# Expert layers: each result row goes straight to its token's place, and the finish reads plain blocks

## The reference, cut to what matters

```
g_val, g_idx = top_k(softmax(t @ w_group + b_group), 1)
e_val, e_idx = top_k(softmax(e_logits of that group), 2);  e_val /= sum(e_val)
weights, expert_id = g_val * e_val, g_idx * 4 + e_idx
hid = silu(t @ w_gate[e]) * (t @ w_up[e]) * combine[t, e]      # width 256
out = sum over the two experts of hid @ w_down[e]
h = layer_norm(alpha * h + out)
```

## Time and profile before

| | |
|---|---|
| median of the runs | 2432.27 us |
| the profiled execution, and its span | 2437.65 us, 2435.8 us |
| PE, DVE, ACT, POOL busy | 93%, 52%, 50%, 9% |
| software queue q0 | 17040 packets, 70.74 MB |
| hardware queue q1 | 50832 packets, 265.57 MB |
| first expert stage, steps | about 1632 to 1832 us |
| second expert stage, steps | about 2193 to 2402 us |

### The profile page before, as it was taken

One profiled execution on the slowest core, in us unless ns is written; L12 is line 12 of the kernel. 1 busy time (PEld: TensorE's weight loads), 2 busy tenths in 40 slices (PEclk: granted clock), 3 DMA queues, 4 the chain that ended last, 5 costly groups with the idle time before them and its releaser, 6 DMA issues.

```text
span 2435.8 us, 29892 instructions
## 1 busy us (share of the span) xinstructions
PE 2272.2 (93%) x11728; PEld 1089.1 (45%) x11728; DVE 1269.0 (52%) x2492; ACT 1224.4 (50%) x2127; POOL 223.7 (9%) x296
## 2 busy tenths in 40 slices
PE   7989999999999999999999999989996999989995
PEld 3333554444443444444444446544333444653333
DVE  5456855556445556776653684643115644653113
ACT  7543656666557566566665863531115664431113
POOL 0000000000000430000000000111221000111231
PEclk9999999999999999999999999989998999989998
DMA  5220011221222210222223231439974131427995
GB/s 194 86 98 9 1 69 70 104 104 72 90 107 79 97 69 36 88 103 104 82 77 131 74 103 54 192 119 384 406 300 156 74 139 39 161 103 310 415 420 234
DMA packets 68012, 338.22 MB, mean 139 GB/s; under 512 B 11702, under 2 KB 12012, under 8 KB 53516
## 3 DMA queue, kind: packets, MB, share of 16 engines
q1 hardware_dynamic: 50832, 265.57, 28.5%
q0 software_dynamic: 17040, 70.74, 7.7%
HBM read 366.62 MB, written 23.10 MB: 160 GB/s over the span
## 4 chain that ended last, share of the span: by engine, by line
PE 79%; DVE 10%; ACT 5%; DMA 3%; issue 3%; POOL 0%; SPq 0%; DVEq 0%; POOLq 0%; ACTq 0%
PE PB L383 11%; PE PB L388 11%; PE PB L389 11%; PE PB L3233 8%; PE PB L3259 4%; PE PB L1670 3%; PE PB L1666 3%; PE PB L1667 3%; PE PB L408 2%; PE PB L409 2%; PE PB L410 2%; PE PB L3185 1%; PE PB L419 1%; DVE WS L320 1%; ACT junk L261 1%
## 5 line engine op out<-in xcount | busy, mean ns | idle before, releaser
L388 PE MATMUL PB<-AS,WS 128*128 128x512 f16 x1416 | 537.0, 379 | 16.7 <-ACT AS L478 12.7
L389 PE MATMUL PB<-AS,WS 128*128 128x512 f16 x1416 | 536.7, 379 | 0.0
L383 PE MATMUL PB<-AS,WS 128*128 128x512 f16 x1416 | 508.4, 379 | 2.6 <-DVE AS L1147 2.5
L320 DVE SCALAR_TENSOR_TENSOR WS<-raw,sc,WS 128x1024 f16<-128x1024 f32 (+3 forms) x288 | 324.7, 1188 | 92.1 <-ACT WS L307 92.1
L307 ACT ACTIVATE WS<-raw,sc 128x1024 f16<-128x1024 f32 (+3 forms) x288 | 284.2, 1056 | 64.6 <-DVE sc L287 64.6
L261 ACT ACTIVATE junk<-raw 128x1024 f16<-128x1024 f32 (+3 forms) x288 | 280.5, 974 | 9.0 <-ACT junk L443 0.4
L3233 PE MATMUL PB<-T 128*64 128x512 f32 x736 | 221.3, 614 | 17.7 <-issue 15.0
L388 PEld LDWEIGHTS PB<-AS,WS 128*128 128x128 f16 x1416 | 138.4, 98 | 196.2 <-ACT AS L478 22.4
L383 PEld LDWEIGHTS PB<-AS,WS 128*128 128x128 f16 x1416 | 138.5, 98 | 172.3 <-DVE AS L1147 4.1
L389 PEld LDWEIGHTS PB<-AS,WS 128*128 128x128 f16 x1416 | 138.5, 98 | 162.8 <-issue 3.0
L3336 ACT ACTIVATE T<-PB 128x256 f32<-128x256 f32 (+1 forms) x32 | 12.1, 377 | 284.2 <-PE PB L3233 274.0
(11 more groups left out here) (627 smaller groups left out, 3483.5 us busy)
## 6 DMA issues: line engine op xcount, KB each, us to landing
T<-in_moe_up SPq DMA_DIRECT2D x26, 2048.0 KB
raw<-in_w_up SPq DMA_DIRECT2D x22, 2048.0 KB, 7.8
T<-in_moe_down SPq DMA_DIRECT2D x26, 1024.0 KB
raw<-in_w_down SPq DMA_DIRECT2D x16, 1408.0 KB, 6.0
raw<-in_w_in_even SPq DMA_DIRECT2D x8, 2048.0 KB, 7.8
raw<-in_w_in_odd SPq DMA_DIRECT2D x8, 2048.0 KB, 7.8
moe_y<-X SPq DMA_DIRECT2D x30, 512.0 KB
WS<-in_moe_up SPq DMA_DIRECT2D x6, 2048.0 KB
```

Source lines behind the costliest of these rows:

```text
L320: e.scalar_tensor_tensor(lo[q], raw[q], s, hi[q], MUL, SUB).then_inc(*k.s("dve_split").up("lo", i, q))
L383: return e.matmul(bank, wh[:, q, c, :], act.lo[c], start=False, stop=c == kt - 1)
L388: e.matmul(bank, wh[:, q, c, :], act.hi[c], start=c == 0, stop=False)
L389: e.matmul(bank, wl[:, q, c, :], act.hi[c], start=False, stop=False)
```

## The change

The store of a block becomes an indirect write by POOL: row numbers `y_i` send each filled row to row 512 * choice + token of `moe_y`, and empty rows (number 2048) are out of bounds and not written. The product of `ids` now carries pair numbers 0 to 1023, so DVE makes two lists from it: `x_i` (minus 512 where the number is 512 or more, which takes one more instruction that the other waits for) and `y_i`. For the single unit of step 3 PE makes the numbers twice (16 matmuls instead of 8), and `y_i` addresses half rows. In the finish SP loads 8 plain blocks of 128 rows. `out_zero`, its memset and `pos_i` are gone; POOL makes a small column `lone` instead. The wait of the copies for the store two steps earlier stays.

```diff
 def moe_sp ...
-        if n > 0:
-            sp_moe_out(k, e, w, layer, n - 1)
-            if n + 1 < NB and experts(n + 1):
-                w.wait_ge(*p.past("down", n - 1))
-                for u in range(2):
-                    sp_moe_down(k, e, w, layer, n + 1, u)
-    sp_moe_out(k, e, w, layer, NB - 1)
+        if n > 0 and n + 1 < NB and experts(n + 1):
+            w.wait_ge(*p.past("down", n - 1))
+            for u in range(2):
+                sp_moe_down(k, e, w, layer, n + 1, u)
     w.wait_ge(*p.past("down", NB - 1))
+    for j in range(2):
+        w.wait_ge(*k.s(f"out_y{j}").past(layer, NB - 1 - (NB - 1 - j) % 2))
+    for q in range(4):
+        for i in range(2):
+            r = S * i + 128 * q
+            e.dma_start(m.y[2 * q + i], k.out_d[layer][r:r + 128, :]).then_inc(*k.s(f"in_y{2 * q + i}").dma(layer))
     sp_load(k, e, w, place(LAST_OUT[layer], 7)[0] + 3)
 moe_dve: ids(b0, b1)
-        e.tensor_scalar(m.x_i[:, b0:b1], PB[7][:, b0:b1], 2048.0, None, ADD).then_inc(*v.up("ids", b0))
+        e.tensor_scalar(m.wrap[:, 0:b1 - b0], PB[7][:, b0:b1], float(S - 2048), float(-S), ALU.is_ge, MUL).then_inc(
+            *v.up("wrap", b0))
+        w.wait_ge(*v.now())
+        e.scalar_tensor_tensor(m.x_i[:, b0:b1], PB[7][:, b0:b1], 2048.0, m.wrap[:, 0:b1 - b0], ADD, ADD).then_inc(
+            *v.up("ids", b0))
...
+        n = min(b1, ORDER[LONE])
+        e.tensor_scalar(m.y_i[:, b0:n], PB[7][:, b0:n], 2048.0, None, ADD).then_inc(*v.up("rows", b0))
+        if n < b1:
+            e.tensor_scalar(m.y_i[:, n:b1], PB[7][:, n:b1], m.lone, 2.0, ADD, MUL).then_inc(*v.up("rows", n))
 moe_pool
+    def store(b):
+        w.wait_ge(*v.past("rows", ORDER[b]))
+        w.wait_ge(*a.past("down", b))
+        w.wait_ge(*v.past("down", b))
+        at = bass.IndirectOffsetOnAxis(m.y_i[:, ORDER[b]:ORDER[b] + 1], 0)
...
+            e.indirect_dma_start(k.out_d[layer], at, m.yst[b % 2], None, bounds_check=2 * S - 1, oob_is_err=False).then_inc(
+                *k.s(f"out_y{b % 2}").dma(layer, b))
     for b in range(NB):
         load_x(b + 2)
...
-    w.wait_ge(*v.past("pos_i"))
...
-    for q in range(4):
-        for i in range(2):
-            at = bass.IndirectOffsetOnAxis(m.pos_i[:, 4 * i + q:4 * i + q + 1], 0)
-            e.indirect_dma_start(m.y[2 * q + i], None, k.out_d[layer], at).then_inc(*k.s(f"in_y{2 * q + i}").dma(layer))
+        if b:
+            store(b - 1)
+    store(NB - 1)
```

More of the change, by code:

```diff
@@ L177, in __init__ @@
         self.gate_d = nc.dram_tensor("mlstm_gates", (16, S), F32, kind="Internal").ap()
-        self.out_d = [nc.dram_tensor(f"moe_y{i}", (16 * 128, D), F32, kind="Internal").ap() for i in range(2)]
+        self.out_d = [nc.dram_tensor(f"moe_y{i}", (2 * S, D), F32, kind="Internal").ap() for i in range(2)]
     def sb(self, name, shape, dt=F32):
@@ L2381, in pool_layernorm @@
     e.iota(m.num.bitcast(I32), [[1, NE]], base=0, channel_multiplier=0).then_inc(*g.up("num_int"))
-    e.iota(m.tok.bitcast(I32), [[128, 4]], base=0, channel_multiplier=1).then_inc(*g.up("tok_int"))
+    e.iota(m.tok.bitcast(I32), [[128, 8]], base=0, channel_multiplier=1).then_inc(*g.up("tok_int"))
     e.memset(m.fresh, 1.0).then_inc(*g.up("fresh", 0))
@@ L2386, in pool_layernorm @@
     e.memset(m.gwr, 0.0).then_inc(*g.up("gain_route_zero"))
-    e.memset(m.xT[0][0:64, :], 0.0).then_inc(*g.up("zero"))
     w.wait_ge(*g.now())
@@ L2395, in pool_layernorm @@
     e.tensor_scalar(m.own, m.num, 64.0, -1.0, MUL, ADD).then_inc(*g.up("own"))
-    e.dma_start(k.out_d[layer][64 * NU - 64:64 * NU, :], m.xT[0][0:64, :]).then_inc(*k.s("out_zero").dma(layer))
+    e.tensor_scalar(m.lone, m.tok[:, 0:1], 64.0, 0.5, ALU.is_ge, MUL).then_inc(*g.up("lone", 0))
+    w.wait_ge(*g.now())
+    e.tensor_scalar(m.lone, m.lone, 2048.0, None, ADD).then_inc(*g.up("lone", 1))
     w.wait_ge(*k.s("in_route").past(layer))
@@ L3073, in moe_at @@
         yst = [k.X[:, 4 + 2 * i:6 + 2 * i, :].rearrange("p a b -> p (a b)") for i in range(2)]
-        num, tok = k.T[:, 49, 0:NE], k.T[:, 49, 32:36]
-        tok16 = k.T[:, 49, 64:66].bitcast(F16)
+        num, tok = k.T[:, 49, 0:NE], k.T[:, 49, 32:40]
+        tok16 = k.T[:, 49, 40:44].bitcast(F16)
+        wrap, lone = k.T[:, 49, 482:486], k.T[:, 49, 486:487]
         one = [k.T[:, 49, 66 + 64 * i:130 + 64 * i].rearrange("p (q e) -> p q e", q=4) for i in range(2)]
@@ L3090, in moe_at @@
         top1, top2, many, den, w1, w2 = (k.small[:, a:a + 4] for a in (132, 136, 140, 144, 148, 152))
-        pos_i, w_i, x_i = (k.small[:, o:o + n].bitcast(U32) for o, n in ((256, 8), (264, NU - NE), (288, NB)))
+        w_i, x_i, y_i = (k.small[:, o:o + n].bitcast(U32) for o, n in ((264, NU - NE), (288, NB), (304, NB)))
         upto, all_ = k.PB[6][:, 0:64], k.PB[6][:, 64:80]
@@ L3118, in moe_sp @@
                 sp_moe_up(k, e, w, layer, n + 2, u)
-        if n > 0:
-            sp_moe_out(k, e, w, layer, n - 1)
-            if n + 1 < NB and experts(n + 1):
-                w.wait_ge(*p.past("down", n - 1))
-                for u in range(2):
-                    sp_moe_down(k, e, w, layer, n + 1, u)
-    sp_moe_out(k, e, w, layer, NB - 1)
-    w.wait_ge(*p.past("down", NB - 1))
-    sp_load(k, e, w, place(LAST_OUT[layer], 7)[0] + 3)
[L3130 to L3140, removed]
+        if n > 0 and n + 1 < NB and experts(n + 1):
+            w.wait_ge(*p.past("down", n - 1))
+            for u in range(2):
+                sp_moe_down(k, e, w, layer, n + 1, u)
+    w.wait_ge(*p.past("down", NB - 1))
+    for j in range(2):
[4 more added lines that the diff above has]
+            e.dma_start(m.y[2 * q + i], k.out_d[layer][r:r + 128, :]).then_inc(*k.s(f"in_y{2 * q + i}").dma(layer))
+    sp_load(k, e, w, place(LAST_OUT[layer], 7)[0] + 3)
 def moe_pe(k, e, w, layer):
@@ L3171, in ids @@
             for i in range(8):
-                x = e.matmul(PB[7][:, b:b + 1], m.onehot[:, i, c:c + 128], m.tok16[:, i % 4:i % 4 + 1], start=i == 0,
-                             stop=i == 7, skip_group_check=True)
+                if b == ORDER[LONE]:
+                    for u in range(2):
+                        x = e.matmul(PB[7][64 * u:64 * u + 64, b:b + 1], m.onehot[:, i, c:c + 64], m.tok16[:, i:i + 1],
+                                     start=i == 0, stop=i == 7, skip_group_check=True)
+                else:
+                    x = e.matmul(PB[7][:, b:b + 1], m.onehot[:, i, c:c + 128], m.tok16[:, i:i + 1], start=i == 0,
+                                 stop=i == 7, skip_group_check=True)
         x.then_inc(*p.up("ids", b1))
@@ L3321, in turn @@
             w.wait_ge(*p.past("up", b - 2))
-        else:
-            w.wait_ge(*k.s("out_zero").past(layer))
         e.activation(m.xT[b % 2][:, 0:512], PB[0][:, :], ACT.Copy).then_inc(*a.up("turn", b))
@@ L3461, in moe_dve @@
     w.wait_ge(*v.now())
-    e.tensor_copy(m.pos_i, m.pos).then_inc(*v.up("pos_i"))
     def match(r, k0, k1, c0=0, c1=S):
@@ L3478, in ids @@
         w.wait_ge(*p.past("ids", b1))
-        e.tensor_scalar(m.x_i[:, b0:b1], PB[7][:, b0:b1], 2048.0, None, ADD).then_inc(*v.up("ids", b0))
+        e.tensor_scalar(m.wrap[:, 0:b1 - b0], PB[7][:, b0:b1], float(S - 2048), float(-S), ALU.is_ge, MUL).then_inc(
[3 more added lines that the diff above has]
+            *v.up("ids", b0))
         for b in range(b0, b1):
             v.mark("ids", b)
+        n = min(b1, ORDER[LONE])
+        e.tensor_scalar(m.y_i[:, b0:n], PB[7][:, b0:n], 2048.0, None, ADD).then_inc(*v.up("rows", b0))
+        if n < b1:
+            w.wait_ge(*k.s(f"pool_{MIXER[layer]}").past("lone", 1))
+            e.tensor_scalar(m.y_i[:, n:b1], PB[7][:, n:b1], m.lone, 2.0, ADD, MUL).then_inc(*v.up("rows", n))
+        for b in range(b0, b1):
+            v.mark("rows", b)
     def turn(b):
@@ L3609, in more @@
         return bass.IndirectOffsetOnAxis(m.w_i[:, 2 * ORDER[n] - NE + u:2 * ORDER[n] - NE + u + 1], 0)
+    def store(b):
[3 more added lines that the diff above has]
+        at = bass.IndirectOffsetOnAxis(m.y_i[:, ORDER[b]:ORDER[b] + 1], 0)
+        if b == LONE:
+            halves = k.out_d[layer].rearrange("r (u c) -> (r u) c", u=2)
+            e.indirect_dma_start(halves, at, m.yst[b % 2][:, 0:512], None, bounds_check=4 * S - 1, oob_is_err=False).then_inc(
+                *k.s(f"out_y{b % 2}").dma(layer, b))
+        else:
+            e.indirect_dma_start(k.out_d[layer], at, m.yst[b % 2], None, bounds_check=2 * S - 1, oob_is_err=False).then_inc(
+                *k.s(f"out_y{b % 2}").dma(layer, b))
     for b in range(NB):
@@ L3625, in moe_pool @@
                                      oob_is_err=False).then_inc(*k.s(f"in_more_down{s}").dma(layer, b + 1))
-    w.wait_ge(*v.past("pos_i"))
-    w.wait_ge(*p.past("down", NB - 1))
-    for j in range(2):
-        w.wait_ge(*k.s(f"out_y{j}").past(layer, NB - 1 - (NB - 1 - j) % 2))
-    for q in range(4):
-        for i in range(2):
-            at = bass.IndirectOffsetOnAxis(m.pos_i[:, 4 * i + q:4 * i + q + 1], 0)
```

(4 more changed lines are left out.)

## The result

| | before | after |
|---|---|---|
| median of 20 runs each | 2434.56 us | 2439.98 us |
| ratio after / before | | 1.0018, 95% interval [1.0011, 1.0025] |
| profiled execution, span | 2437.65, 2435.8 us | 2441.27, 2439.5 us |
| all DMA | 338.22 MB | 329.85 MB |

The forecast was 2420 and "faster"; the kernel became 0.18% slower. 8.37 MB less are moved, and the time went up. Ratios and intervals use only executions in the fast state; one of before (2518.6 us) and one of after (3961.62 us) were not.

The account below looks back on a forecast made before the run. PE, busy 93% of the span, was taken as held by late weights and by idle transfer chains at stage ends. 2437.65 - 3.4 - 11.6 + 3.0 = 2425.7 us profiled, 2420 as median; range 2411 to 2430.

Parts of the forecast that it names:

- Part A: End of both expert stages: indirect store and plain loads take 9.2 us per end, gaining 3.4 us in all.
- The estimate of 7 us: Gain at the two stage ends by the Trainium skill's fit: store 2.3 us, first 1 MB of loads 4.4.
- Part C: Stores issued by POOL in q0 delay gathers and weights: cost 1.5 us per stage, 3.0 in all, bounds -1 and 8.
- the store of step 1, issued some 4 us before it, is nearly through by then: 0.8 us: In q0, the gather for step 5 has no slack, but the older store ahead costs it only 0.8 us.
- rival 2: Gathers starve behind stores in q0, with waits at steps 5 and 8 of both stages: 2440 us, slower, chance 0.10.
- Part B: Late in the stages, fewer store bytes and better transfer order: 8.6 us gained in the second, 3.0 first, 11.6 in all.
- can come that much earlier: Second stage, step 15: 2.66 MB less stored brings its weights 6.4 us earlier; 2.0 us of its wait gained.
- The order term: Late second stage: step 10's down weights go up to 1.6 us earlier with nothing ahead; their 1.85 us wait goes.

## Why the prediction was wrong

**Part A, the finish: right.** Forecast 9.2 us per end and 3.4 saved in all; measured 8.5 per end and 4.4 saved, and 3.2 us by the ratio (0.5 to 5.6) where it is done alone. The estimate of 7 us that stands beside the forecast was too high: it has 2.3 us for the store and 4.4 for the first two loads, by a fit for POOL's DMAs though SP issues the loads, and in the second stage they took 3.3 us (2407.04 to 2410.36) and 5.1 (2410.36 to 2415.48).

**Part C, the queue: wrong, and it decides the sign.** The step that failed is "the store of step 1, issued some 4 us before it, is nearly through by then: 0.8 us". I took the bytes' time from the earlier trace rows and forgot the time between issue and first byte, and the near-empty packets of step 3's down load, which POOL issues 1.3 us before the store. After the store's issue at 2230.59 q0 passed 63 packets without data up to 2236 (DMA queues of after, 2230 to 2236 us, first line), and the store's bytes in the 7 us after that (2236 to 2243 us, second line):

```profile
q0 software_dynamic: 63, 0.00, 0.6%
q0 software_dynamic: 212, 0.49, 18.0%
```

So all of the store's 0.48 MB was still ahead when the gather was issued at 2234.52. The wait was 6 us per stage, with 1.6 us of slow matmuls behind it in the first stage and 2.3 in the second. Before lost 3.3 and 2.5 us around this step to late weights and rows, and all but 0.2 of that is gone. The net cost is 4.6 and 5.7 us, 10.3 in all; I had 3.0, with 8 as the bound.

My rival 2 had the mechanism and, by luck, the time (2440): it expected a second wait at step 8 that didn't come, and it took 15.0 us of gains where there were some 7. Of the 4.4 and 5.4 us that the gather lost, the runs give 2.3 and 0.9 to the store's bytes and the rest to an empty store ahead, where it had 5.2 us of bytes. I gave it 0.10 since the store ahead was "older": its age was right and said nothing.

**Part B, the bytes and the order: wrong too.** Of the 11.6 us after's trace shows 2.2, all in the first stage (forecast 3.0); the late waits and slow matmuls of the second stage, forecast to give 8.6, are 13.5 us in both kernels, and 13.7 with the gathers first, so part C is not the reason. The step that failed is that the weights of step 15 "can come that much earlier" by the bytes saved: the waits of steps 10 and 13 went, but 3.0 us came on top before step 11, 1.59 before step 14, and step 15 kept its own.

What the runs show of the price: in q1 the bytes are worth some 0.9 us per MB over both stages, so the change's 8.37 MB would give 7.6 us there. The order term is negative where full stores stay in q1. But the bytes were not taken out of q1 alone: the filled rows went into q0, beside the overflow weights and gathers, and what is saved by skipping empty rows there is 3.9 us. A single price per MB is not to be had: in q0 the empty rows give 0.5 us per MB, the filled ones 1.1 (8.8 us for 8.08 MB), each uncertain by some 0.4.

**The sum by the trace**, in us: around step 5 +10.3, late part -2.2 (first stage) and 0.0 (second), matmuls of step 0 -0.9, ends -4.4: +2.8, where the profiled executions differ by 3.6.

**The sum by the runs**, in us from the ratios: full stores into q0 +15.6; empty rows skipped -3.9; that leaves -7.3 for the new finish and the indirect form together, to come to the +4.4 measured. The finish is 3.2 of it by its ratio and 5.9 by its trace. The remaining 4.1 or 1.4 us are within the noise, since each ratio here is uncertain by 2.6 to 3.7 us; that the indirect form gains anything is not shown. What keeps the wait before step 15 stays open (4.20 us in before, 4.75 in after, 4.86 and 4.92 with the gathers first): it was 2.80 with the finish alone, and 3.18 or 2.79 where nearly no result rows are written.

**The better kernel.** With the gathers first and step 10's down weights later, the change is worth having: 0.9967 of before, about 0.5% less than after. Most of that is the place of the gathers.

## What to carry to other kernels

A transfer that moves to another queue stands ahead of what follows it there, from its issue until its last byte; find the load with no slack in that queue and put it first. Price a queue by packets and by the delay to the first byte, since rows that are skipped save the bytes alone. Don't count on later slack for time that PE loses early in a double-buffered stage, because the next loads start when PE frees their buffers. And read waits from the engine's own timeline: a chain of waits that runs through a long transfer hides what the engine waited for meanwhile.

## What the runs showed of the hardware

- With both queues full, q0 and q1 pass packet for packet: after's 2243 to 2251 us had 225 packets of q0 with 0.79 MB and 220 of q1 with 2.54 MB. A queue's share of the bytes is set by the size of its packets.

```profile
q1 hardware_dynamic: 220, 2.54, 74.4%
q0 software_dynamic: 225, 0.79, 24.3%
```

- The Trainium skill (DMA: Bandwidth & Descriptors, section "Queues, rings and completion order") says that an engine drains a whole packet, typically of some 9 to 17 descriptors, before it switches. The counts here are those of the profile's packets, 144 for 128 rows, and the totals of the two queues are equal. On which engine a packet ran, and after how many of them an engine switches, isn't shown.
- A row that an indirect transfer skips still passes as a near-empty packet: the store of 29 rows and the one of 128 both passed 144.
- With q1 full, after's q0 passed nothing from 2228 to 2233 us although its down load was issued at 2229.31, and a gather of 0.5 MB took 11.3 to 12.6 us with no store ahead.
- A store on idle engines lands in 2.58 us with 29 filled rows and 3.33 with all 128 by indirect write, 2.60 for the plain one with 128 (second stage, chain of waits).
- POOL sometimes issues late: after's up load of step 14 came 3.94 us after the instruction before it, some 1.5 later than at the steps beside it, where it waits for PE alone; the kernel with the gathers first has 3.97 at the same place. What held it isn't shown.

```profile
2356.54 1.00 POOL L3634 DMA_INDIRECT T<-in_moe_up,small  x1 [3.94 <-issue]
```
